# Attention of block one in pairs of heads, one query tile a step, with half-size product pieces between

## The reference, cut to what matters

```python
for l in range(2):
    h = rms_norm(x, attn_norm_g[l]); z = h @ w_in[l]
    qa, ka, va, qb, kb, vb, ga, gb = split(z)
    qa, ka = rope(rms_norm(qa)), rope(rms_norm(ka))      # 8 heads, 2 kv heads, 64 wide
    ya = window_gqa(qa, ka, va, sink[l]) @ w_proj_a[l]   # |key - query| <= 128, and a sink
    qb, kb = rms_norm(qb), rms_norm(kb)                  # 8 heads, 64 wide
    yb = neighbourhood_attn(qb, kb, vb, rel_bias[l]) @ w_proj_b[l]  # 2-d window and bias
    x = x + (sigmoid(ga) * ya + sigmoid(gb) * yb) @ w_out[l]
    x = x + (silu(rms_norm(x) @ w_gate[l]) * (rms_norm(x) @ w_up[l])) @ w_down[l]
```

## Time and profile before

| | us |
|---|---|
| median of 3 runs | 3805.82 |
| profiled execution | 3810.24 |
| its span | 3808.4 |
| TensorE busy (matmul) | 3525.1 |
| VectorE busy | 2164.8 |
| ScalarE busy | 1197.5 |
| GpSimd busy | 557.0 |

### The profile page before, as it was taken

The page is one execution under the profiler, slowest core; times in us unless marked ns, Lnnn a source line. Parts: engine busy times, 40 slices in busy tenths (PEclk is TensorE's granted clock), DMA queues, the critical chain, the costliest instruction groups (busy, mean ns, idle before and its releaser), DMA issues. The chain is left out here.

```text
span 3808.4 us, 38430 instructions
## 1 busy us (share of the span) xinstructions
PE 3525.1 (93%) x15368; PEld 2781.5 (73%) x15368; DVE 2164.8 (57%) x2690; ACT 1197.5 (31%) x1503; POOL 557.0 (15%) x459
## 2 busy tenths in 40 slices
PE   6889999999899999978988998999899889989997
PEld 4667878886677778856776785888666767858885
DVE  6744476546643466444787435654568874355545
ACT  3433332233333322213222322433333233223332
POOL 1011231121111222111000111100010001111000
PEclk9998999999998999989999999999999999999999
DMA  3112345321121445321111222222211112212221
GB/s 113 43 35 57 126 184 194 143 95 67 33 58 49 160 179 196 122 97 61 67 56 50 70 97 79 100 91 98 78 67 67 50 50 79 99 67 89 100 100 56
DMA packets 72177, 344.41 MB, mean 90 GB/s; under 512 B 25152, under 2 KB 26048, under 8 KB 35648
## 3 DMA queue, kind: packets, MB, share of 16 engines
q1 hardware_dynamic: 70272, 339.51, 25.7%
q0 software_dynamic: 432, 1.28, 0.1%
q10 hardware_dynamic: 1296, 1.16, 0.1%
HBM read 340.51 MB, written 2.10 MB: 90 GB/s over the span
## 5 line engine op out<-in xcount | busy, mean ns | idle before, releaser
L730 PE MATMUL bank_b<-Hhi_b,whi_b 128*128 128x512 f32 x2976 | 1228.2, 413 | 128.9 <-POOL Hlo_b L810 42.9
L731 PE MATMUL bank_b<-Hlo_b,whi_b 128*128 128x512 f32 x2976 | 1179.0, 396 | 0.0
L732 PE MATMUL bank_b<-Hhi_b,wlo_b 128*128 128x512 f32 x2976 | 1177.9, 396 | 0.0
L709 DVE TENSOR_TENSOR wlo_b<-raw_b,whi_b 128x2048 fp32r<-128x2048 f32 (+2 forms) x290 | 627.2, 2163 | 569.5 <-ACT whi_b L703 569.3
L730 PEld LDWEIGHTS bank_b<-Hhi_b,whi_b 128*128 128x128 f32 x2976 | 572.0, 192 | 280.8 <-issue 107.6
L731 PEld LDWEIGHTS bank_b<-Hlo_b,whi_b 128*128 128x128 f32 x2976 | 572.5, 192 | 125.3 <-issue 12.6
L732 PEld LDWEIGHTS bank_b<-Hhi_b,wlo_b 128*128 128x128 f32 x2976 | 570.3, 192 | 124.8
L703 ACT ACTIVATE whi_b<-raw_b 128x2048 fp32r<-128x2048 f32 (+2 forms) x290 | 511.4, 1764 | 397.9 <-PE bank_b L732 397.8
L730 PE MATMUL bank_b<-Uhi_b,whi_b 128*128 128x512 f32 x1024 | 408.1, 399 | 0.0
L732 PE MATMUL bank_b<-Uhi_b,wlo_b 128*128 128x512 f32 x1024 | 401.7, 392 | 0.0
L731 PE MATMUL bank_b<-Ulo_b,whi_b 128*128 128x512 f32 x1024 | 401.6, 392 | 0.0
(11 more groups left out here) (207 smaller groups left out, 3574.2 us busy)
## 6 DMA issues: line engine op xcount, KB each, us to landing
raw_b<-in_w SPq DMA_DIRECT2D x234, 1024.0 KB, 4.8
ada_b<-in_wada SPq DMA_DIRECT2D x48, 1024.0 KB, 6.9
raw_b<-in_w SPq DMA_DIRECT2D x40, 512.0 KB, 3.7
raw_b<-in_w SPq DMA_DIRECT2D x16, 768.0 KB, 4.3
rel_b<-in_rel SPq DMA_DIRECT2D x128, 24.0 KB, 2.4
X_keep<-in_x SPq DMA_DIRECT2D x4, 512.0 KB, 9.3
out<-X_keep SPq DMA_DIRECT2D x8, 256.0 KB, 2.0
cond_b<-in_c SPq DMA_DIRECT2D x2, 512.0 KB, 4.4
```

Of the source, the lines that this page charges most:

```text
L709: self.nc.vector.tensor_tensor(self.wlo[n % RAW_SLOTS][:, 0:words], self.raw[n % RAW_SLOTS][:, 0:words], self.whi[n % HI_SLOTS][:, 0:words ...
L730: self.nc.tensor.matmul(out, whi[:, k, cols], xhi, start=(k == 0), stop=False)
L731: self.nc.tensor.matmul(out, whi[:, k, cols], xlo, start=False, stop=False)
L732: mm = self.nc.tensor.matmul(out, wlo[:, k, cols], xhi, start=False, stop=(k == nk - 1))
```

## The change

- A step is now a pair of heads `(2g, 2g+1)` and one query tile: 32 steps (`STEPS`) with softmax state for a pair. Scores of the two heads are issued alternately, and so are their value matmuls. In between, the list is: scores of step i, a slot, exponentials of i, transposes of i-1, a slot, scaling of i, value matmuls of i-1.
- All transposes are evacuated by ScalarE. The sink's exponential has an input of its own (`ns`, one more small VectorE instruction). Score buffers are six of 384 columns in place of two of 1280; there are four `pt` buffers, not three.
- Pieces of the input projection and of the first gate branch are half as large (2 blocks, 6 matmuls). `paced` spreads them evenly: 40 over the slots of the first 16 steps, 48 over 30 slots of the last 16. 8 half-size pieces go ahead of the first step.
- The biases of two heads are built together at the end of a pair, and loaded by pairs.
- At the start, the second panel is split and the tables are made ahead of the sums of squares and of the first product, for all engines but ScalarE, which makes the sines (`sines`) after its squares. TensorE's wait for all nine inputs moves ahead of the first product. Cosine and sine have scratch of their own.

```diff
-    def lazy_product(self, n, nk, width, cols, rhs, then=None):
+    def lazy_product(self, n, nk, width, cols, rhs, then=None, size=4):
...
+    s.split_ahead(1)
+    s.add("tables")
     for c in range(DC):
         rms_sum(s, 0, "attn", c)
+    s.add("sines")
...
+        def paced(slots):
+
+            total, done = len(todo), 0
+            for i in range(1, slots + 1):
+                while done < -(-total * i // slots):
+                    gap()
+                    done += 1
+                yield
+            while True:
+                yield
...
+        pace = paced(2 * HALF)
+        for i in range(len(STEPS) + 1):
+            if i == HALF:
                 gap(len(todo))
                 while lag:
                     finish(lag.pop(0))
+                load_bias_pair(A_HEADS // 2)
+                bias_pair(A_HEADS // 2)
+            if i < len(STEPS):
+                g, t = STEPS[i]
+                for h in (2 * g, 2 * g + 1):
+                    s.temp("sc", 6, ("sc", l, h, t))
                     s.small.take(("score", l, h, t))
+                s.add("score", l, i)
+                next(pace)
+                s.add("soft", l, i)
+            if i == HALF + 1:
+                n = mix_pieces(s, todo, n, l, 0, 2)
+                pace = paced(2 * HALF - 2)
+            if i >= 1:
+                before = STEPS[i - 1]
+                if before[1] == 0:
+                    s.long.take(("y", l, before[0]))
+                for h in (2 * before[0], 2 * before[0] + 1):
+                    s.temp("pt", 4, ("pt", l, h, before[1]))
+                    s.small.take(("tp", l, h, before[1]))
+                s.add("tp", l, i - 1)
+                next(pace)
+            if i < len(STEPS):
+                s.add("soft2", l, i)
+            if i >= 1:
+                s.add("pv", l, i - 1)
+                if before[1] == TT - 1:
+                    s.add("evy", l, before[0])
+            if i < len(STEPS) and t == TT - 1 and A_HEADS // 2 <= g < 7:
+                bias_pair(g + 1)
...
+                    for j, tile in enumerate(tiles):
+                        for h in heads:
+                            V, col = (VA, 64 * (h // 4)) if i < HALF else (VB, 64 * (h - A_HEADS))
+                            mm = nc.tensor.matmul(k.out_of(y)[64 * (h % 2):64 * (h % 2) + 64, ktile(t)], V[:, tile, col:col + 64],
+                                                  pt[slot("pt", ("pt", l, h, t))][:, ktile(j)],
+                                                  start=(j == 0), stop=(j == len(tiles) - 1))
```

More of the change, by code:

```diff
@@ L332, in schedule_one @@
[L332 to L347, removed]
@@ L656, in token_tiles, with pair @@
     return (t - 1, t, t + 1), 128
-SC_AT = (0, 256, 640, 1024)
+STEPS = tuple((g, t) for g in range(8) for t in range(TT))
+HALF = len(STEPS) // 2
+def pair(i):
+    g, t = STEPS[i]
+    return (2 * g, 2 * g + 1), t
 class Common:
@@ L1039, in _ @@
                 elif kind == "soft2":
[L1040 to L1045, removed]
+                    l, i = a
+                    heads, t = pair(i)
+                    pool.wait_ge(*after("rec", l, i))
+                    for j, h in enumerate(heads):
+                        p = scores_of(l, h, t)
+                        nc.gpsimd.tensor_scalar(p, p, rec[:, i % 2, j:j + 1], 1.0, ALU.mult, ALU.mult)\
                             .then_inc(*mark("pool", ("p", l, h, t)))
@@ L1065, in _ @@
             for kind, *a in s.items:
-                if kind == "tables":
+                if kind == "sines":
                     act.wait_ge(rest_landed, 16 * NREST)
@@ L1287, in _ @@
                 elif kind == "score":
-                    l, h, t = a
+                    l, i = a
+                    heads, t = pair(i)
                     tiles, at = token_tiles(t)
                     n = len(tiles) * P
[L1291 to L1298, removed]
-                            dve.wait_ge(*after("bm", l, h))
-                        if h >= 2:
-                            dve.wait_ge(*after("nm", l, h - 2))
@@ L1303, in _ @@
[L1303 to L1316, removed]
-                elif kind == "soft2":
[L1318 to L1324, removed]
-                            .then_inc(*mark("dve", ("den", l, h)))
-                        dve.wait_ge(*after("den", l, h))
-                    nc.vector.reciprocal(rec[:, h % 2], den[:, h % 2]).then_inc(*mark("dve", ("rec", l, h)))
-                elif kind == "tp" and a[2] % 2 == 0:
-                    evacuate_pt(dve, *a)
@@ L1470, in _ @@
-                    pe.wait_ge(*after("pt", l, h, t))
-                    out = k.out_of(y)[64 * (h % 2):64 * (h % 2) + 64, ktile(t)]
-                    for i, j in enumerate(tiles):
-                        mm = nc.tensor.matmul(out, V[:, j, col:col + 64], pt[slot("pt", ("pt", l, h, t))][:, ktile(i)],
-                                              start=(i == 0), stop=(i == len(tiles) - 1))
-                    names = [("free", ("pt", l, h, t))] + ([y] if h % 2 == 1 and t == TT - 1 else [])
```

209 lines of the change are left out of this document (121 added, 88 removed).

## The result

The changed kernel takes 3834.05 us, the median of four runs (3832.47 to 3838.95); the kernel before took 3804.56 beside it (3799.25 to 3810.64). The ratio is 1.0079, with an interval of [1.0061, 1.0097]: slower by 0.8%, and clear of no change, where 3759 and faster was forecast. The profiled execution took 3835.18 (span 3833.3), 25 more than that of before.

What follows compares the result with a forecast made beforehand. TensorE, busy 93% of the span, was taken as the bound, so gains come from waits, low clock and packing. Start -6.7, first halves -3.7 and -6.7, second halves -17 twice: -51 from 3810.24, so 3759; range 3710 to 3815.

Steps and rivals of the forecast that it cites:

- Packing, 0.85 a step: Attention scores and values: two heads' neighbouring matmuls overlap in the array, saving 0.85 us a step, between bounds 0 and 1.1.
- The second halves, 118: Second half of attention, a layer: 135.0 us before becomes 132 without packing and 118 with it.
- Hidden: Second half: ScalarE's chain to evacuated transposes, 3.8 us, fits within 5.0 of cover; only 4 gate columns are late, 9 us.
- SyncE's bias loads go as pairs, 16 issues at once, with three panels in flight as cover: Second half: SyncE issues a pair's bias loads in one block, covered by panels in flight; no cost was added.
- clock 1.0: Second halves: sign of a right forecast, a time near 118 us with TensorE at full granted clock.
- The first halves, 144: First half of attention, a layer: 147.7 and 150.7 us before become 144 packed, 155 unpacked.
- About 4 us idle: First half: TensorE waits about 4 us for transposes behind a chunk's VectorE chain; ready at 7.7, scaled tiles by 13.1.
- rival C: Attention: chunks' chains hide; first halves 55 + 16 x 2.5 + 9 + 4 = 108 us; 3663 in full, about 3710 at half; chance 0.12.
- I take 0.9 each: First half: low clock behind 8 waits of 4 us costs 0.9 us each, 7 us a layer.
- Rival D: First halves: low clock at every chunk, 3.2 us for each of 16 in two layers, +37; 3846 without packing; chance 0.13.
- The start, -6.7: Start of the kernel: bank wait of 9.95 us goes, first normalisation at 46.2 not 52.88; bounds +7.4 to -10.
- VectorE makes the tables from 25 to 35: Start: VectorE's tables took 11.8 us before, with a 2 us wait for ScalarE that two scratch tiles remove.

Runs made afterwards that it cites:

- Heads apart: Changed kernel plus evacuation before exponentials, two-step depth, head-by-head bias loads and chunks finished in two parts, with the two heads' matmuls kept apart: 3771.5 us, ratio 0.9909.
- Evacuation first: Changed kernel with exponentials of step i listed behind transposes of step i-1, so ScalarE evacuates the transposes first: 3809.4 us, ratio 1.0004.
- depth alone: Changed kernel with transposes and value matmuls two steps behind the scores, exponentials still ahead of the evacuation: 3857.8 us, ratio 1.0132.
- both: Changed kernel with transposes and values two steps behind the scores and the evacuation ahead of the newest exponentials: 3742.7 us, ratio 0.9835.

## Why the prediction was wrong

**Packing, 0.85 a step: right.** Heads apart gives about 0.87 of overlap. That overlap takes place was reasoned; that the size agrees to 0.02 is partly luck, for 0.85 was a choice between 0 and 1.1. The Trainium skill ("TensorE: Matmul & The Clock Gate", Part 3: Packing small matmuls) says that different row or column groups run concurrently, and the traces agree. Its sentence that a weight load overlaps only when the row group differs is not what was measured: value pairs share all rows, and twelve records took 0.88 where twelve one after the other would have taken about 1.5.

**The second halves, 118: failed by 18 us each (136.1, 136.3).** The forecast was 106 of work, 12 of waits and nothing for the clock. Two steps failed. The first is "Hidden" and what follows it: a chain of 3.8 against 5.0 of cover, late only at four gate columns for 9 us. I gave the evacuation its place behind the exponentials on ScalarE and took the slack for real; the waits there were 21.1 us in 8 places. Evacuation first takes 9.7 and 7.7 out. The second is "SyncE's bias loads go as pairs, 16 issues at once, with three panels in flight as cover": I named the block and priced it at nothing. Spreading it takes 7.0 and 6.8 out. A term was missing as well: behind the waits came the low clock, where I expected "clock 1.0" and the window has 0.92. By the trace's clock TensorE was busy for 17 us of the half at the lower level, so some 8 us were lost, an estimate. Together the two edits take 31.2 us out, waits and clock, of the 36.4 missing. They are not quite the same microseconds, since the forecast had allowed 12 us of waits a half.

**The first halves, 144: failed by 15.8 and 16.6.** The mechanism was right, one chunk at a time ahead of a row sum that TensorE needs within one step; two terms of the sum were too small. "About 4 us idle" was up to 6.5, and TensorE's waits came to 43.5 us in a half; the forecast had 33 of them in its 137, with 104 of work (the terms of rival C without its last 4). And "I take 0.9 each", 7 us for the low clock, was scaled down from a single row of before. By the trace's clock TensorE was busy for 42 us of the first half at the lower level, so it lost some 21 us (8 and 12 before): an estimate, and the largest part of the miss. What is left for the work is then 94, 10 less than forecast. The reading that nothing was lost "behind shorter ones" was wrong too: the kernel before has clock 0.89 in its second half, where this is TensorE's longest wait:

```profile
PE bank_b L1458 <- DVE mx_b L1306: 2.9, 2, 1.9
```

Rival D put the low clock at every chunk, at 3.2 each, 26 us a half. It was the right rival, with 0.13: with packing kept, its +37 on the forecast gives 3796, and the second halves add the rest.

The forecast set its halves against 147.7 and 135.0, windows that are cut behind the scores of head 9. Its gains by half (-3.7 and -17) therefore say little each; their sum is not touched by it.

**The start, -6.7: failed.** The first normalisation begins at 51.26, not 46.2 (before 52.88). "VectorE makes the tables from 25 to 35" took until 40.1. These rows show why:

```profile
22.41 11.19 POOL L1041 TENSOR_TENSOR qa_b<-qa_b,sq_b 128x512 f32<-128x512 f32 x7 [21.95 <-ACT sq_b L1103]
...
26.51 1.40 DVE L859 TENSOR_SCALAR tab_b<-tab_b 128x512 f32<-128x512 f32 x1
...
35.71 0.42 DVE L859 TENSOR_SCALAR tab_b<-tab_b 128x512 f32<-128x512 f32 x1
...
40.23 0.68 DVE L1215 TENSOR_SCALAR EQ_b<-bank_b 128x512 f32<-128x512 f32 x1
...
44.11 0.80 PE L756 MATMUL bank_b<-Hhi_b,whi_b 128*128 128x512 f32 x1 [3.78 <-ACT qn_b L1138]
```

The same instruction lasts 1.40 while GpSimd adds, and 0.42 once it is done. The two ran one after the other before; the change put them side by side. So the bank wait shrank to 3.78 and did not go. The start alone, in the kernel before, has the same 1.40 and won only 0.6 us, so nothing in the new attention is behind it.

The three terms, 32.4, 36.4 and 5.1 us, are 73.9 of the 76.2 between the forecast and the profiled execution. One error stands behind the waits. I checked each chain alone against TensorE's cover, and priced the ordered queues in front of it (ScalarE's exponentials, VectorE's chunks, SyncE's block) by their best case; the lower clock that came with the waits then cost about as much again. I had even written that depth was one step, no longer a head, and took that for 4 us.

## What to carry to other kernels

When a change cuts the distance between producer and consumer, go through each in-order queue between them and write down what stands ahead of the consumer's input at the new distance. Fix that order before adding depth: depth alone cost 24 us here, the order alone won 25, both won 91. A saving in TensorE's work is worth its size only where TensorE doesn't wait. The packing was all there in this change, some 0.87 us a step, and the second halves got 12 us shorter; in the first, waits and the low clock behind them took back more than the whole change had won.

## What the runs showed of the hardware

- Matmuls of two heads that are neighbours in the queue and use different rows, or different columns, of the array overlap without being alternated: scores took 0.71 us alternated and 0.72 head after head, values 0.88 and 1.15. One head's scores alone took the same 0.71.
- VectorE's instructions on a 128x512 float32 tile with one input took 1.40 us beside GpSimd's additions and 0.42 to 0.43 without them, and GpSimd's seven additions took 11.19 and not 9.87. It is not so for every pair: a reduction beside GpSimd's scaling at 114.31 took 0.62, as elsewhere.
- TensorE's lower clock level came with waits of under 2 us as well: 0.89 in the second half of the kernel before, with no wait above 1.9.
- Small DMA issues add up: sixteen took 10.2 us of SyncE's queue, and ScalarE waited 7.7 for the half-size panel behind them.
